# Attention in rounds of two key tiles and units of one query block, with maxima per unit, sums split by engine and four banks of logits

## The chip, the cores and the metric

The kernel runs on one core of a Trainium2 chip. The metric is the device time of one launch in microseconds. TensorE is PE, VectorE DVE, ScalarE ACT, GpSimd POOL and SyncE SP, as in the profile; DMAs are issued by SP, ACT or POOL.

## The reference

The whole is a two-layer decoder: a gated-DeltaNet layer, a shared projection of K, V and forget gates, and a forgetting-attention layer (batch 1, 2048 tokens, width 1024). The change lies in the attention of the second layer, 16 heads of 64:

```python
for blk in range(seq // B_BLOCK):
    s0 = blk * B_BLOCK
    s1 = s0 + B_BLOCK
    logits = (jnp.einsum('bhqd,bhkd->bhqk', q[:, :, s0:s1], k[:, :, :s1]).astype(jnp.float32)
              + log_f_cum[:, :, s0:s1, None] - log_f_cum[:, :, None, :s1])
    causal = jnp.arange(s0, s1)[:, None] >= jnp.arange(s1)[None, :]
    p = jax.nn.softmax(jnp.where(causal, logits, -jnp.inf), axis=-1)
    outs.append(jnp.einsum('bhqk,bhkd->bhqd', p.astype(v.dtype), v[:, :, :s1]))
o = jnp.concatenate(outs, axis=2).transpose(0, 2, 1, 3).reshape(bsz, seq, B_W)
return (o * jax.nn.silu(z)) @ w_out
```

## The kernel before

The program is a row of stages, each ending in a barrier of all engines: DeltaNet projection (pa), delta rule (dr), output projection (oa), the K/V projection (pk), the query projection (pb), the attention (at) and the last output projection (ob). The function `attention` is the attention stage. It works on 8 pairs of heads. For a pair, logits are computed transposed, 128 keys on the partitions by up to 512 queries: a tile is one key tile (kb) against one query block (qb of 4). A pair has 40 tiles (16 + 12 + 8 + 4), and each is done for both heads: 640 exact logits in all.

An exact logit (`exact_logits`, lines 1977 to 1986) is two float32r matmuls (L1983 with the high parts, the gates and minus the maximum as extra rows; L1986 with the low parts) and, on the diagonal, a bf16 mask matmul (L1985). ACT takes the exponential (L2123) into `probs`. One step later PE multiplies the probabilities with V (`sum_values`, L1997): float32 matmuls that fill 64 columns each, one head on each half; the trace shows four records per tile. The denominators are sums over key tiles, added up on DVE (even tiles and all of block 0: L2059, L2062) and POOL (odd tiles: L1870, L1873), joined on DVE (L2069), and then summed over the partitions by PE with a matrix of ones (`sum_tiles`, L2010). ACT inverts them by logarithm and exponential (L2128, L2130). DVE multiplies the output with the gate Z (L2076) and with the inverse (L2081).

The maximum that is subtracted is a rough one. `rough_logits` (L1948, mask L1951) computes queries by keys from the high parts only, 80 of them per pair, each up to 128 x 512, and DVE reduces each to a column of `partial` (L1960). When all 80 are there, DVE reduces them to `top` (L1965), PE turns it (L1971), ACT negates it (L1975) and POOL places it as a row of Q1 by two DMAs (L1855).

The order of the work is written out by hand. In every step j (one tile) each engine does its part of tile j or a few before. `max_steps` spreads the 80 rough logits of the next pair over steps 6 to 33 of the present one: one after each head's exact logits, the rest after the values. For the first pair all 80 run before the main loop (`alone`), and they may use the banks of `logits` as well. The banks of PSUM are: logits 2, rough 2, o 2, total 1, top_turned 1. `probs` holds three tiles. Blocks go from the last (qb = 3) to the first. SP loads a pair's K, Q, V and Z in four blocks of 512 tokens, each block in a group of loads for the rough logits (`load_one`, `load_gates`, L1889 and L1893) and one for the rest (`load_two`, L1904); pair p + 2 takes over the buffers of pair p block by block once that block is gated.

Of the kernel before, what the change touches and what calls it, by code (L numbers as in the profile page):

```python
# [12 lines left out]

# [14 lines left out]
P = 128  # L28
# [3 lines left out]
BLK = 512  # L32
# [1728 lines left out]
def attention(nc, s_K, s_Fp, s_V, s_Q, s_ZT, s_u2T):  # L1761

# [10 lines left out]
    MAIN = [(qb, kb) for qb in reversed(range(NB)) for kb in range(NQ * (qb + 1))]  # L1773
    MAXI = [(qb, h, sub, grp) for qb in range(NB) for h in range(2) for sub in range(NQ) for grp in range(qb + 1)]
    STEPS, MAXS = len(MAIN), len(MAXI)
    ENDS = [j for j in range(STEPS) if j == STEPS - 1 or MAIN[j][0] != MAIN[j + 1][0]]

    ON_POOL = [(j, h) for j in range(STEPS) for h in range(2) if MAIN[j][0] and MAIN[j][1] % 2]
    ON_DVE = [(j, h) for j in range(STEPS) for h in range(2) if (j, h) not in ON_POOL]
    MAX_START, MAX_END = 6, STEPS - 6  # L1780
    with Stage(nc, "at") as st:
# [5 lines left out]
        probs = st.sb("probs", [P, 3, 2, BLK])  # L1787
        sum_v, sum_g = st.sb("sum_v", [P, 2, 2, BLK]), st.sb("sum_g", [P, 2, BLK])
        partial = st.sb("partial", [P, 2, NT, NB])
        top = st.sb("top", [P, 2 * NT])  # L1790
        minus_top = st.sb("minus_top", [2 * NT, P], F32R)
        inv, u = st.sb("inv", [P, BLK]), st.sb("u", [P, 2, BLK])
# [5 lines left out]
        top_in = st.pool_sem("top_in")  # L1798
        consts = st.sem("consts")
        rows_set = [st.sem(f"rows_set{s}") for s in range(2)]  # L1800
        ev = lambda n, per, credit=0: Event(st, n, per, credit)
        logits_ok, probs_ok, pv_ok = ev("logits_ok", 2 * STEPS), ev("probs_ok", 2 * STEPS, 2), ev("pv_ok", STEPS, 3)
        v_summed, g_summed = ev("v_summed", len(ON_DVE), 6), ev("g_summed", len(ON_POOL))
        joined, total_ok = ev("joined", 2 * (NB - 1), 2), ev("total_ok", NB, 2)
# [7 lines left out]
        def over_pairs(body):  # L1812

            for p in range(PAIRS):
                body(p, p // 2, p % 2, p < PAIRS - 1)
# [11 lines left out]
        def _(pool):  # L1827
# [20 lines left out]
            for s in range(2):  # L1848
                pool.sem_inc(u_stored[s], 16)
# [351 lines left out]
```

## Time and profile before

| what | value |
|---|---|
| median of 3 runs | 3534.41 us (3532.44 to 3536.05) |
| the profiled execution's own time | 3540.65 us |
| its span in the trace | 3539.0 us |
| attention stage in it, about | 2417 to 3322 us |
| main loop of the attention, first exact logits to last sum over partitions | 2482 to 3315 us |
| granted clock of TensorE over the span | 0.949 of full speed |

The profile is one execution of the program. Times in its timeline are microseconds from the span's start. "Busy" of PE counts from a matmul's start to its modelled end, and matmuls overlap, so the distance from one start to the next tells more than the length. An engine's idle time stands before the instruction that ended it, with what released it.

### The profile page before, as it was taken

Reading aid. Unit: us, or ns where it says so; the run is one execution under the profiler, and the core shown is the slowest. Engines: PE = TensorE matmul, PEld = TensorE weight load, DVE = VectorE, ACT = ScalarE, POOL = GpSimd, SP = SyncE. Lnnn points to the kernel's source line nnn. Section 1 sums busy time; section 2 is a strip of 40 time slices with the busy share of each in tenths; the row PEclk is TensorE's granted clock in tenths of the full one; section 3 lists DMA queues with packets and bytes.
Section 4 is the critical chain, followed back from the end, with each engine's and each line's share of the span. In section 5 each row is a group of like instructions: output and inputs, shape, how many; then the busy total and the mean of one; then the engine's idle time right before and its main releaser. Section 6 shows DMA issues by size and latency. Waiting matters only on the chain. (4 is left out here: it accounts for less than half of the span.)

```text
span 3539.0 us, 41132 instructions
## 1 busy us (share of the span) xinstructions
PE 3193.6 (90%) x15158; PEld 2315.6 (65%) x15158; DVE 1756.8 (50%) x2771; ACT 1218.3 (34%) x2078; POOL 940.8 (27%) x739
## 2 busy tenths in 40 slices
PE   5889899999978997978999699996999999999798
PEld 4666566888867886866888578884444444444476
DVE  4454444566645665544211142115676777675433
ACT  4344445444414453224111131110344444444311
POOL 0578860233235440100000000001333333333210
PEclk8999899999989998988999899996999999999899
DMA  5233422567555654555431244317243433330333
GB/s 204 74 118 101 131 91 61 187 209 223 177 154 192 200 182 147 180 163 158 119 83 48 87 145 116 107 48 173 60 108 81 108 84 79 81 84 10 110 128 119
DMA packets 270102, 436.35 MB, mean 123 GB/s; under 512 B 73214, under 2 KB 170118, under 8 KB 259612
## 3 DMA queue, kind: packets, MB, share of 16 engines
q1 hardware_dynamic: 230812, 332.18, 31.8%
q0 software_dynamic: 23520, 86.21, 7.8%
q10 hardware_dynamic: 15600, 15.73, 1.5%
q8 instruction: 101, 1.65, 0.2%
q14 instruction: 69, 0.57, 0.1%
HBM read 283.10 MB, written 150.82 MB: 123 GB/s over the span
## 5 line engine op out<-in xcount | busy, mean ns | idle before, releaser
L2123 ACT ACTIVATE at_probs<-at_logits 128x512 f32<-128x512 f32 (+3 forms) x640 | 331.2, 532 | 414.0 <-PE at_logits L1986 381.7
L173 PE MATMUL pa_y<-pa_h_high,pa_w_high 128*128 128x512 f32 x1056 | 422.6, 400 | 7.5 <-ACT pa_acc L839 5.5
L1960 DVE TENSOR_REDUCE at_partial<-at_rough 128x1 f32<-128x512 f32 (+1 forms) x600 | 349.8, 605 | 129.1 <-PE at_rough L1948 76.3
L174 PE MATMUL pa_y<-pa_h_low,pa_w_high 128*128 128x512 f32 x1056 | 413.0, 391 | 0.0
L175 PE MATMUL pa_y<-pa_h_high,pa_w_low 128*128 128x512 f32 x1056 | 412.7, 391 | 0.0
L1873 POOL TENSOR_TENSOR at_sum_g<-at_sum_g,at_probs 128x512 f32<-128x512 f32 (+2 forms) x240 | 251.0, 1063 | 381.1 <-ACT at_probs L2123 380.0
L1997 PE MATMUL at_o<-at_probs,at_V 128*64 128x512 f32 (+3 forms) x1280 | 305.2, 555 | 2.9 <-ACT at_probs L2123 2.9
L1948 PE MATMUL at_rough<-at_K,at_Q 66*128 66x512 f32 (+1 forms) x600 | 250.1, 423 | 30.4 <-DMA at_K<-s_Fp 22.4
L1983 PE MATMUL at_logits<-at_Q,at_K 67*128 67x512 f32 (+3 forms) x640 | 260.9, 408 | 13.4 <-DMA at_Q<-at_minus_top 8.4
L1986 PE MATMUL at_logits<-at_Q,at_K 128*128 128x512 f32 (+3 forms) x640 | 254.0, 397 | 0.0
L173 PE MATMUL pk_y<-pk_h_high,pk_w_high 128*128 128x512 f32 x544 | 218.4, 401 | 30.4 <-POOL pk_ident L98 27.9
L173 PEld LDWEIGHTS pa_y<-pa_h_high,pa_w_high 128*128 128x128 f32 x1056 | 199.5, 189 | 59.8 <-issue 12.3
L173 PE MATMUL pb_y<-pb_h_high,pb_w_high 128*128 128x512 f32 x512 | 204.8, 400 | 35.9 <-POOL pb_ident L98 31.6
L1948 PEld LDWEIGHTS at_rough<-at_K,at_Q 66*128 66x128 f32 x600 | 117.6, 197 | 181.2 <-DVE at_partial L1960 142.2
L174 PEld LDWEIGHTS pa_y<-pa_h_low,pa_w_high 128*128 128x128 f32 x1056 | 199.5, 189 | 43.9 <-issue 3.8
L175 PEld LDWEIGHTS pa_y<-pa_h_high,pa_w_low 128*128 128x128 f32 x1056 | 199.3, 189 | 42.1
L175 PE MATMUL pk_y<-pk_h_high,pk_w_low 128*128 128x512 f32 x544 | 217.3, 399 | 0.0
L174 PE MATMUL pk_y<-pk_h_low,pk_w_high 128*128 128x512 f32 x544 | 217.3, 399 | 0.0
L1983 PEld LDWEIGHTS at_logits<-at_Q,at_K 67*128 67x128 f32 x640 | 123.2, 192 | 135.5 <-ACT at_probs L2123 89.2
L2062 DVE TENSOR_TENSOR at_sum_v<-at_sum_v,at_probs 128x512 f32<-128x512 f32 (+3 forms) x288 | 164.5, 611 | 92.9 <-ACT at_probs L2123 92.9
L174 PE MATMUL pb_y<-pb_h_low,pb_w_high 128*128 128x512 f32 x512 | 204.3, 399 | 0.0
L175 PE MATMUL pb_y<-pb_h_high,pb_w_low 128*128 128x512 f32 x512 | 204.2, 399 | 0.0
(348 smaller groups left out, 5685.8 us busy)
## 6 DMA issues: line engine op xcount, KB each, us to landing
at_Q<-s_Q SPq DMA_DIRECT2D x96, 256.0 KB, 6.8
s_qkv<-pa_sil POOLq DMA_DIRECT2D x16, 1024.0 KB, 6.6
pa_sil<-s_qkv SPq DMA_DIRECT2D x16, 1024.0 KB, 6.3
dr_kv<-s_qkv SPq DMA_DIRECT2D x16, 1024.0 KB
s_K<-pk_parts SPq DMA_DIRECT2D x32, 512.0 KB, 8.0
s_Q<-pb_parts SPq DMA_DIRECT2D x32, 512.0 KB, 8.0
at_K<-s_K SPq DMA_DIRECT2D x32, 512.0 KB, 5.7
pa_wraw<-in_a_w_in_dram ACTq DMA_DIRECT2D x15, 1024.0 KB
```

What stands on the lines that cost most here:

```text
L173: nc.tensor.matmul(out, w_high[:, k], h_high[:, k], start=k == 0, stop=False)
L174: nc.tensor.matmul(out, w_high[:, k], h_low[:, k], start=False, stop=False)
L175: ins = nc.tensor.matmul(out, w_low[:, k], h_high[:, k], start=False, stop=k == KC - 1)
L1873: ins = g.tensor_tensor(sum_g[:, h, off:BLK], sum_g[:, h, off:BLK], x, ALU.add)
L1948: ins = nc.tensor.matmul(bank[:, 0:width], Q1[s][0:DH + 2, h, q_at], K1[s][0:DH + 2, h, grp * BLK:grp * BLK + width], start=True, stop=grp ...
L1960: reduced.done(nc.vector.tensor_reduce(partial[:, h, qb * NQ + sub, grp:grp + 1], rough_bank(j, alone)[:, 0:width], AX.X, ALU.max))
L1983: nc.tensor.matmul(out, K1[s][0:DH + 3, h, k_at], Q1[s][0:DH + 3, h, q_at], start=True, stop=False)
L1986: logits_ok.done(nc.tensor.matmul(out, K2[s][:, h, k_at], Q2[s][:, h, q_at], start=False, stop=True))
L1997: ins = nc.tensor.matmul(o[at, m % 2, off:BLK], V[s][:, kb, at], probs[:, j % 3, h, off:BLK], start=kb == 0, stop=kb == NQ * (qb + 1) - 1)
L2062: ins = v.tensor_tensor(to, to, x, ALU.add)
L2123: probs_ok.done(nc.scalar.activation(probs[:, j % 3, h, off:BLK], logits[:, h, off:BLK], ACT.Exp))
```

## The change

`attention` is rewritten. The unit of work is one query block of one pair (32 units, `UNITS`): the pair 0 goes from block 0 to block 3, the others from 3 to 0. A unit is made of rounds of two key tiles (160 rounds). In a round PE computes the four exact logits (two tiles by two heads), each in a bank of its own, and then the values of the round before, eight records without anything between. The maxima are those of a unit, not of a pair: after a unit's last rough logit they are reduced to `top`, turned into the bank of `total` (there is none for `top_turned` any more), negated, and placed by ACT with two DMAs. Only the eight rough logits of unit 0 run ahead. A planner's loop (`ROUGHS`) spreads the others over the rounds so that a unit's are done four rounds before it starts, as evenly as their due times allow; they stand behind the exact logits in up to four groups. Head 0 is summed on DVE, head 1 on POOL, both tiles of a round; a unit's first two tiles are added directly. The partition sum takes head 0 from `sum_v` and head 1 from `sum_g`, so nothing is joined. `o` has one bank instead of two and `inv` two buffers instead of one. The last product (`normalize`) moves from DVE to POOL. In the stage's start, the rows of ones are filled in parts, and SP issues the first blocks' loads in the order of their use.

```diff
-    MAIN = [(qb, kb) for qb in reversed(range(NB)) for kb in range(NQ * (qb + 1))]
-    MAXI = [(qb, h, sub, grp) for qb in range(NB) for h in range(2) for sub in range(NQ) for grp in range(qb + 1)]
...
-    MAX_START, MAX_END = 6, STEPS - 6
+    UNITS = [(p, qb) for p in range(PAIRS) for qb in (range(NB) if p == 0 else reversed(range(NB)))]
+    START = [0]
+    for _, qb in UNITS:
+        START.append(START[-1] + 2 * (qb + 1))
...
+    ITEMS = [(u, h, sub, grp) for u, (_, qb) in enumerate(UNITS) for h in range(2) for sub in range(NQ) for grp in range(qb + 1)]
+    FIRST = 2 * NQ
+    ITEM_END = [2 * NQ * sum(qb + 1 for _, qb in UNITS[:u + 1]) for u in range(len(UNITS))]
+
+    ROUGHS, DONE = [], FIRST
+    for R in range(ROUNDS):
+        due = [(ITEM_END[u] - DONE, max(START[u] - 4, 0)) for u in range(1, len(UNITS)) if ITEM_END[u] > DONE]
+        take = max([-(-n // (d - R + 1)) for n, d in due if d >= R], default=0)
+        ROUGHS.append(range(DONE, DONE + take))
+        DONE += take
+    TURN = {u: 1 + next(R for R in range(ROUNDS) if ITEM_END[u] - 1 in ROUGHS[R]) for u in range(1, len(UNITS))}
...
-        logits, rough = st.ps("logits", [P, 2, BLK]), st.ps("rough", [P, 2, BLK])
-        o = st.ps("o", [P, 2, BLK])
-        total, top_turned = st.ps("total", [P, BLK]), st.ps("top_turned", [P, BLK])
+        logits, rough = st.ps("logits", [P, 4, BLK]), st.ps("rough", [P, 2, BLK])
+        o, total = st.ps("o", [P, BLK]), st.ps("total", [P, BLK])
...
+            for R in range(ROUNDS + 3):
+                for u in ended(R, 2):
+                    normalize(u)
+                if R < ROUNDS:
+                    add_up(R)
...
+            for n in range(NB):
+                load_one(sp, 0, n)
+                if n < 2:
+                    sp.wait_ge(rows_k, n + 1)
+                load_gates(sp, 0, n)
+                if n:
+                    load_two(sp, 0, n - 1)
...
+                fetch = [] if p + 2 >= PAIRS else [qb] if p else reversed(range(NB)) if qb == NB - 1 else []
...
+            def sum_values(R):
+                u = UNIT_OF[R]
+                p, qb = UNITS[u]
+                if R == START[u]:
+                    gated.wait(pe, u - 1)
+                probs_ok.wait(pe, 4 * R + 3)
+                for t, kb, off in tiles(R):
                     for h in range(2):
...
+            for R in range(ROUNDS + 2):
+                if R < ROUNDS:
...
+                    if R == START[u]:
+                        for n in range(qb + 1):
+                            pe.wait_ge(two_in[p % 2][n], (p // 2 + 1) * TWO)
+                        pe.wait_ge(top_in, 32 * (u + 1))
+                    part = -(-len(items) // 4)
+                    for t, kb, off in tiles(R):
+                        for h in range(2):
+                            exact_logits(R, t, kb, off, h)
+                            for j in items[(2 * t + h) * part:(2 * t + h + 1) * part]:
...
+                                rough_logits(j)
+                for summed in ended(R, 1):
+                    sum_tiles(summed, turned)
+                if 1 <= R <= ROUNDS:
+                    sum_values(R - 1)
+                for turned in turned_in(R):
+                    turn_top(turned, summed)
...
+            for R in range(ROUNDS + 2):
+                for u in ended(R, 1):
+                    gate(u)
+                if R < ROUNDS:
+                    items, first = ROUGHS[R], R == START[UNIT_OF[R]]
+                    half = 2 * -(-len(items) // 4)
+                    for j in items[:half]:
+                        reduce(j)
+                    if not first:
+                        add_up(R, 0)
+                    for j in items[half:]:
+                        reduce(j)
+                    if first:
+                        first_two(R)
+                    else:
+                        add_up(R, 1)
...
+                for h in range(2):
+                    act.dma_start(Q1[p % 2][DH + 2:DH + 3, h, columns(qb)].bitcast(F32), minus_top[h * NQ:(h + 1) * NQ].bitcast(F32))\
+                       .then_inc(top_in, 16)
...
+                    if R >= 2:
+                        pv_ok.wait(act, R - 2)
+                        v_summed.wait(act, ADDED[R - 2] - 1)
+                        g_summed.wait(act, ADDED[R - 2] - 1)
```

PE's order before, two steps with rough logits in the middle of a pair (at_logits exact, at_rough rough, at_o values):

```order
L1997 MATMUL at_o<-at_probs,at_V 64x512 x2
L1948 MATMUL at_rough<-at_K,at_Q 128x512
L1983 MATMUL at_logits<-at_Q,at_K 128x512
L1986 MATMUL at_logits<-at_Q,at_K 128x512
L1948 MATMUL at_rough<-at_K,at_Q 128x256
L1951 MATMUL at_rough<-at_mask_q,at_ident_b 128x128
L1983 MATMUL at_logits<-at_Q,at_K 128x512
L1986 MATMUL at_logits<-at_Q,at_K 128x512
L1948 MATMUL at_rough<-at_K,at_Q 128x512
L1997 MATMUL at_o<-at_probs,at_V 64x512 x2
```

PE's order in the change, from the last exact logit of a unit's second round on:

```order
L1960 MATMUL at_logits<-at_Q,at_K 128x512
L1963 MATMUL at_logits<-at_Q,at_K 128x512
L1948 MATMUL at_rough<-at_K,at_Q 128x128
L1951 MATMUL at_rough<-at_mask_q,at_ident_b 128x128
L1988 MATMUL at_total<-at_sum_v,at_ones 64x512
L1988 MATMUL at_total<-at_sum_g,at_ones 64x512
L1974 MATMUL at_o<-at_probs,at_V 64x512 x4
L1994 MATMUL at_total<-at_ident,at_top 8x128
L1960 MATMUL at_logits<-at_Q,at_K 128x512
```

The values of one tile stood between the exact logits of two steps; now those of two tiles stand together, with the partition sums ahead of them and the turned maxima behind.

DVE's order before, in steps with rough logits (at_partial reductions, at_sum_v adds of both heads of every other tile):

```order
L1960 TENSOR_REDUCE at_partial<-at_rough 128x1 x2
L2062 TENSOR_TENSOR at_sum_v<-at_sum_v,at_probs 128x512 x2
L1960 TENSOR_REDUCE at_partial<-at_rough 128x1 x5
L2062 TENSOR_TENSOR at_sum_v<-at_sum_v,at_probs 128x512 x2
L1960 TENSOR_REDUCE at_partial<-at_rough 128x1 x6
```

DVE's order in the change, the rounds at the start of a unit:

```order
L2039 TENSOR_REDUCE at_partial<-at_rough 128x1 x4
L2054 TENSOR_TENSOR at_sum_v<-at_probs 128x512
L2070 TENSOR_TENSOR at_u<-at_o,at_Z 128x512
L2039 TENSOR_REDUCE at_partial<-at_rough 128x1 x2
L2062 TENSOR_TENSOR at_sum_v<-at_sum_v,at_probs 128x512
L2039 TENSOR_REDUCE at_partial<-at_rough 128x1 x2
L2062 TENSOR_TENSOR at_sum_v<-at_sum_v,at_probs 128x512
```

An add of one head stands between the second and the third reduction of every round, and another behind the fourth.

## Rows read from the trace of the kernel before

**Rows 1.** The page, busy time, share of the span and instructions of each engine.

```profile
PE 3193.6 (90%) x15158; PEld 2315.6 (65%) x15158; DVE 1756.8 (50%) x2771; ACT 1218.3 (34%) x2078; POOL 940.8 (27%) x739
```

**Rows 2.** Three stretches: length, busy time of each engine, granted clock, DMA share, GB/s.

```profile
2440.00:2450.00 10.00, 10.00 (x28) 5.86 (x26) 10.00 (x20) 0.00 (x0) 0.00 (x0) 0.50 1.09 273
2482.00:2500.00 18.00, 17.79 (x57) 7.82 (x57) 5.06 (x10) 8.04 (x14) 6.25 (x6) 0.78 0.42 100
2605.00:3220.00 615.00, 602.75 (x2770) 298.13 (x2769) 450.93 (x811) 264.62 (x505) 213.02 (x219) 1.00 0.32 80
```

**Rows 3.** Timeline of PE, one step: start, length, line, tiles, count.

```profile
2602.02 0.50 PE L1983 MATMUL at_logits<-at_Q,at_K 67*128 67x512 f32 x1
2602.36 0.40 PE L1986 MATMUL at_logits<-at_Q,at_K 128*128 128x512 f32 x1
2602.60 0.40 PE L1983 MATMUL at_logits<-at_Q,at_K 67*128 67x512 f32 x1
2602.83 0.40 PE L1986 MATMUL at_logits<-at_Q,at_K 128*128 128x512 f32 x1
2603.17 1.08 PE L1997 MATMUL at_o<-at_probs,at_V 128*64 128x512 f32 x4
2604.18 0.50 PE L1983 MATMUL at_logits<-at_Q,at_K 67*128 67x512 f32 x1
```

**Rows 4.** Timeline of PE, values followed by the sum over partitions.

```profile
3270.07 1.08 PE L1997 MATMUL at_o<-at_probs,at_V 128*64 128x512 f32 x4
3270.97 1.03 PE L2010 MATMUL at_total<-at_sum_v,at_ones 128*64 128x512 f32 x4
```

**Rows 5.** Timeline of PE, one rough logit between two exact ones.

```profile
3213.27 0.40 PE L1948 MATMUL at_rough<-at_K,at_Q 66*128 66x512 f32 x1
3213.51 0.40 PE L1983 MATMUL at_logits<-at_Q,at_K 67*128 67x512 f32 x1
```

**Rows 6.** Timeline of PE, the turned maxima of the last two pairs that have them.

```profile
3115.70 0.28 PE L1971 MATMUL at_top_turned<-at_ident,at_top 128*32 128x128 f32 x1
...
3222.47 0.28 PE L1971 MATMUL at_top_turned<-at_ident,at_top 128*32 128x128 f32 x1
```

**Rows 7.** Timeline of PE, the wait in the third step of a block.

```profile
3234.03 0.50 PE L1983 MATMUL at_logits<-at_Q,at_K 67*128 67x512 f32 x1 [0.72 <-ACT at_probs L2123]
```

**Rows 8.** Groups of the stage by shape: count, busy us, mean ns, idle before.

```profile
L1960 DVE TENSOR_REDUCE at_partial<-at_rough 128x1 f32<-128x512 f32 x420 | 280.5, 685 | 86.0 <-PE at_rough L1948 76.3 <-PE at_rough L1951 7.7
...
L2123 ACT ACTIVATE at_probs<-at_logits 128x512 f32<-128x512 f32 x448 | 258.9, 596 | 284.1 <-PE at_logits L1986 272.8 <-DVE at_sum_v L2059 0.5
...
L1873 POOL TENSOR_TENSOR at_sum_g<-at_sum_g,at_probs 128x512 f32<-128x512 f32 x144 | 182.6, 1288 | 239.3 <-ACT at_probs L2123 239.3
...
L2062 DVE TENSOR_TENSOR at_sum_v<-at_sum_v,at_probs 128x512 f32<-128x512 f32 x192 | 128.3, 708 | 68.4 <-ACT at_probs L2123 68.4
```

**Rows 9.** Timeline, POOL adds and the VectorE product beside them.

```profile
2643.26 2.52 POOL L1873 TENSOR_TENSOR at_sum_g<-at_sum_g,at_probs 128x512 f32<-128x512 f32 x2 [5.93 <-ACT at_probs L2123]
...
2644.97 1.36 DVE L2081 TENSOR_TENSOR at_u<-at_u,at_inv 128x512 f32<-128x512 f32 x1
```

**Rows 10.** Timeline, the stage's start until the first exact logits.

```profile
2425.80 1.16 SPq L1893 DMA_DIRECT2D at_K<-s_Fp  x4
...
2429.80 0.45 PE L1948 MATMUL at_rough<-at_K,at_Q 66*128 66x128 f32 x1 [22.45 <-DMA at_K<-s_Fp]
...
2473.43 0.40 PE L1971 MATMUL at_top_turned<-at_ident,at_top 128*32 128x128 f32 x1 [1.79 <-DVE at_top L1965]
...
2482.21 0.76 PE L1983 MATMUL at_logits<-at_Q,at_K 67*128 67x512 f32 x1 [8.39 <-DMA at_Q<-at_minus_top]
```

**Rows 11.** Timeline of PE, the last sum over partitions.

```profile
3315.28 1.08 PE L2010 MATMUL at_total<-at_sum_v,at_ones 128*64 128x512 f32 x4
```

**Rows 12.** Timeline of VectorE, the first of its two fills with ones.

```profile
2418.02 3.47 DVE L2047 MEMSET at_K<- 3x4096 f32 x1 [53.67 <-PEq L56]
```

**Rows 13.** DMAs of the maxima (line 1855), from issue to landing.

```profile
DMA to landing us min/median/max: 1.7/1.8/7.0
```

More of the change, by code:

```diff
@@ L14 @@
+import itertools
 import math
@@ L1826, in _, with tiles, columns @@
+        def tiles(R):
+            r = R - START[UNIT_OF[R]]
+            qb = UNITS[UNIT_OF[R]][1]
+            return [(t, 2 * r + t, max(0, 2 * r + t - qb * NQ) * P) for t in range(2)]
+        def columns(n):
+            return slice(n * BLK, (n + 1) * BLK)
         @block.gpsimd
@@ new lines, in _ @@
+            load_two(sp, 0, NB - 1)
+            for n in range(NB):
+                load_one(sp, 1, n)
+            sp.wait_ge(rows_next, 2)
+            for n in range(NB):
+                load_gates(sp, 1, n)
+            for n in range(NB):
+                load_two(sp, 1, n)
+            for u, (p, qb) in enumerate(UNITS):
+                fetch = [] if p + 2 >= PAIRS else [qb] if p else reversed(range(NB)) if qb == NB - 1 else []
+                for n in fetch:
+                    gated.wait(sp, u)
+                    for part in (load_one, load_gates, load_two):
+                        part(sp, p + 2, n)
+                u_ok.wait(sp, u)
+                sp.dma_start(s_u2T[p * P:(p + 1) * P, columns(qb)], u_buf[:, u % 2]).then_inc(u_stored[u % 2], 16)
@@ new lines, in free_total, with sum_tiles @@
+            def free_total(u, turned):
+                logged.wait(pe, u)
+                minus_ok.wait(pe, turned)
+            def sum_tiles(u, turned):
+                v_summed.wait(pe, ADDED[START[u + 1] - 1] - 1)
+                g_summed.wait(pe, ADDED[START[u + 1] - 1] - 1)
+                free_total(u - 1, turned)
+                for h, x in enumerate((sum_v, sum_g)):
+                    ins = nc.tensor.matmul(total[h * DH:(h + 1) * DH], ones[:, :], x[:, u % 2], start=True, stop=True)
+                total_ok.done(ins)
@@ new lines, in add_up, with gate @@
+            def add_up(R, t):
+                u, n = UNIT_OF[R], ADDED[R] - ADDS[R]
+                off = tiles(R)[t][2]
+                probs_ok.wait(dve, 4 * R + 2 * t)
+                v_summed.wait(dve, n + t - 1)
+                to = sum_v[:, u % 2, off:BLK]
+                v_summed.done(v.tensor_tensor(to, to, probs[:, R % 2, t, 0, off:BLK], ALU.add))
+            def gate(u):
+                p, qb = UNITS[u]
+                pv_ok.wait(dve, START[u + 1] - 1)
+                dve.wait_ge(two_in[p % 2][qb], (p // 2 + 1) * TWO)
+                if u >= 2:
+                    dve.wait_ge(u_stored[u % 2], 16 * (u // 2))
+                gated.done(v.tensor_tensor(u_buf[:, u % 2], o[:, :], Z[p % 2][:, columns(qb)], ALU.mult))
@@ L2103, in _ @@
         @block.scalar
         def _(act):
+            a = nc.scalar
             act.preload_act_table_set("natural_log_exp_and_others")
[L2106 to L2133 removed]
```

431 lines of the change are left out of this document (162 added, 269 removed).

## The prediction

> **What bounds the kernel now.** The page comes first: PE is busy for 90% of the span, no other engine for more than half [rows 1]. The change touches the attention stage alone, so the stretches come next. In steady state the granted clock is 1.00 (2.4 GHz) and PE is busy 602.75 of 615 us, idle 2%, while DVE is busy 73%, ACT 43% and POOL 35% [rows 2]. That PE is busy need not mean that it does useful work, so the third view is the timeline of PE: what is the distance from start to start? The first float32r logit after the values takes 0.34 us to the next start, the second and third 0.24 and 0.23, the last one before the values 0.34, the four value matmuls 1.01 [rows 3]. Values that are followed by more float32 work on half the columns take 0.90 [rows 4]. So each passage into the values and back costs (0.34 - 0.24) + (0.34 - 0.24) + (1.01 - 0.90) = 0.31 us that no wait explains; I take 0.30, since the distances are read to 0.01. A pair with rough logits takes 3222.47 - 3115.70 = 106.77 us [rows 6]. The stage's main loop is bound by PE's order of work, not by a wait. Its prologue isn't: for 80 rough logits PE runs at a clock of 0.50 (1.2 GHz) and DVE is busy without a gap, 20 reductions in 10 us [rows 2].
>
> **Part 1, rounds of two tiles.** There are 40 tiles per pair and 8 pairs, so 320 passages now, and 160 with two tiles' values standing together (the order shows x4 where x2 stood). 160 x 0.30 = **-48 us**, all of it on PE. Sums over partitions that now stand behind a rough logit have edges of their own; always standing ahead of the values they have none. I estimate half of the 32, 16 x 0.30 = **-5 us**. The matmuls themselves are as many as before.
>
> **Part 2, four banks for logits.** PE waits 0.72 us for ACT in the third step of a block [rows 7], once per pair by the repeating pattern. With four banks a logit waits for the exponential four back, which in a round of about 5 us is long done: ACT needs 4 x 0.60 = 2.4 us [rows 8]. 8 x 0.7 = **-6 us**. The 12 us of idle PE in 615 [rows 2] bound what all waits together give: 17 us over the loop's 833 us [rows 10, 11].
>
> **Part 3, the start.** Now the first rough logit starts at 2429.80, some 4 us after the gates' transfers are issued at 2425.80; these stood behind two fills of 3.47 us on DVE [rows 10, 12]. A fill of a quarter of that row takes 0.9 us, and the loads of block 0 need about 6 us from 2417: first rough logit at about 2425. Eight of them with their reductions take 5 us at this clock (0.50 us each [rows 2], plus the start). Turning, negating and placing the maxima takes 8.8 us, 2473.43 to 2482.21, with the queues full [rows 10], and they will be full again. So the first exact logits start at about 2439, not 2482.2: **-43 us**. The 72 rough logits that are no longer in front are now PE's work inside: 0.24 us each [rows 5], about 0.25 with those that need a mask: **+18 us**. The planner's loop, worked through, puts 16, 12, 12, 6, 6, 5, 5, 5, 5 of them into the first nine rounds and then 4 per round up to round 137. Rounds 0 to 2 are therefore bound by DVE: 40 reductions and 6 adds, near 27 us, and round 2 waits for the maxima of unit 1, turned only at the end of round 1, another 8.8 us. Round 3 runs at the low clock still: the clock came back about 8 us after dense work began ((1 - 0.78) x 18 / 0.5 = 8 us at the lower level [rows 2]). That is 46 us for four rounds whose content on PE at the full clock is 27 us (6.4 for the two rounds of unit 0, 8.0 for two full ones, 46 x 0.25 for the rough logits, 0.9 for a sum over partitions); the present start loses 4 us in that way. **+15 us**. Rounds with 5 or 6 rough logits put two behind one logit and so wait about 1 us for a bank: **+6 us**. The start as a whole gives -4 us only.
>
> **Part 4, one bank for o and smaller units.** The maxima are turned 32 times, not 8: 24 x 0.1 us (from the 0.04 to the next start and the 0.28 of length [rows 6] as bounds): **+2 us**. The single bank of o makes the first values of a unit wait for the gate of the last. The gate's turn on DVE comes right after the previous values end, and PE has a whole round of logits ahead of these values, 3 us or more against a product of 0.7: nothing on the path; uncovered it would cost 32 x 0.7 = 22 us. ACT now issues the transfers of the maxima and waits for the turn at a round's end; that delays its next exponential by about 1.5 us and is covered by the 2.6 us that ACT has free per round (uncovered: 31 x 1.5 = 46 us). Between DMAs of 1.8 us median [rows 13] and the maxima's three rounds of lead nothing waits after round 6. SP fetches pair 2 once unit 3 is gated, 8 MB in about 35 us, for rough logits 8 rounds (40 us) later: just in time. The tail gets **+1 us**: POOL's product takes 1.29 us [rows 8] for DVE's 0.7.
>
> **Part 5, sums by engine.** DVE gets head 0 and POOL head 1 of every tile. By count DVE gains: no joins, no final product. But timing changes. In the trace a DVE product with two SBUF inputs that starts at 2644.97, while POOL's adds run until 2645.78, ends at 2646.33: it takes 1.36 us instead of 0.68, and ends 0.55 after POOL [rows 9]. All 28 rows of such DVE operations with more than 0.72 us per instruction lie beside a POOL add. The Trainium skill, "SBUF — State Buffer", section "SBUF: two separate sides", says that the pair of ports which VectorE and GpSimd share is an exclusive lock, held for the whole instruction, and that a VectorE operation with two SBUF inputs takes it. By that rule, the trace agrees, each add that meets one of POOL's would wait out its rest. In a full round with 4 rough logits PE needs 8 x 0.24 + 4 x 0.25 + 4 x 0.45 + 0.30 = 5.0 us; DVE needs 4 reductions at 0.50 [rows 2] to 0.55 and 2 adds at 0.7 [rows 8], 3.5 us. Followed step by step, the first add starts while POOL sums the first tile of head 1 and waits about 1 us, the second finds POOL idle: 4.5 us, under 5.0. The unknown is bounded by 0 and by two full waits of 1.27 per round, which would make DVE's round 6.0 us. I take a small toll, **+6 us**.
>
> Sum: -48 - 5 - 6 - 43 + 18 + 15 + 6 + 2 + 1 + 6 = **-54 us**, against the profiled execution's 3540.65 us (3539.0 in its span). The median of the runs is 6 us lower, 3534.4, so the prediction is 3534.4 - 54 = **3480 us**. A measurement of this kernel can tell about 0.2%, 7 us, from no change.
>
> **The rivals.**
> - *The clock stays low in the start.* While DVE sets the pace in the first rounds PE may not count as dense, as it didn't for 50 us in the prologue [rows 2]. If it stays at 0.50 to round 10, some 45 us of content take about 25 us more, since part of it waits anyway: 3505 us. For: rounds of 5 and 6. Against: these rounds are bound by PE at the low clock. 0.14.
> - *The passage isn't what the distances say.* If only entering and leaving are saved and the two tiles' values cost 1.01 each (rows 4 have other weights behind the values, not another tile's), each round saves 0.20: 32 us less 48 is 16 us lost: 3496 us. 0.10.
> - *Better than the sum.* The rounds of the start overlap more, the waits of PE vanish altogether (17 us instead of 6) and the toll of part 5 is zero: 3463 us. 0.15.
> - *The shared port makes DVE the bound: slower.* It decides from a mean wait of (5.0 - 3.5) / 2 = 0.75 us per add; 54 us are eaten up over 130 rounds at 0.4 more per round, so at 0.95. With 1.15 per add the round is 5.8 us, 130 x 0.8 = 104 us: 3584 us. PE would then wait for rough banks. For: POOL now works in every round, with two adds of 1.27 [rows 8]. Against: a wait of DVE gives POOL time to finish, so two full waits in each round don't hold together. 0.06.
> - *No change*, by the start turning out 40 us worse: 0.03.
>
> **The numbers.** The forecast, 3470 to 3495 us, has 0.52. Faster by over 0.2%: 0.52 + 0.14 + 0.10 + 0.15 = 0.91, same 0.03, slower 0.06. The range for 8 in 10 reaches from the better case to beyond the first rival: 3459 to 3515 us.
>
> **What the profile will show.** The four value matmuls as one group of eight per round, 1.9 us from start to next start, and 160 of them; pairs that take 98 to 99 us between their qb = 3 units instead of 106.77; first exact logits near 2439; the clock at 0.50 until about 2482; DVE adds of two lengths, near 0.65 and up to 1.9; PE's idle under 2% after round 9. The forecast is wrong if pairs take more than 102 us: then either the passages kept their price, or PE waits for reductions behind adds that POOL holds. It is also wrong if the clock is low beyond 2500.

## The result and the profile after

The changed kernel takes 3478.27 us (median of 4 runs, 3476.47 to 3482.47) against 3535.23 us of the kernel before on the same chip (4 runs, 3532.44 to 3538.62): ratio 0.984, 95% interval 0.9823 to 0.9857. That is 57 us less; 54 us less and 3480 us were forecast.

The page's busy line stands to [rows 1] so: PE's busy time falls by 60 us and the span by 58, so its share stays at 90%; POOL has 99 us more to do.

```profile
PE 3133.1 (90%) x15182; PEld 2334.9 (67%) x15182; DVE 1769.4 (51%) x2659; ACT 1226.4 (35%) x2102; POOL 1039.4 (30%) x764
```

Stretches of the kernel after, with the columns of [rows 2] (length, busy us of PE, PEld, DVE, ACT, POOL with counts, granted clock, DMA share, GB/s): rounds 0 and 1, the wait for the maxima of unit 1, rounds 2 and 3, then the clock's rise, then the steady part.

```profile
2434.24:2448.51 14.27, 12.52 (x36) 7.76 (x37) 7.74 (x15) 2.17 (x4) 1.28 (x2) 0.50 1.09 249
2448.51:2462.54 14.03, 12.39 (x38) 6.67 (x37) 9.30 (x19) 1.32 (x4) 1.18 (x2) 0.51 1.08 213
2462.54:2470.53 7.99, 0.28 (x3) 0.11 (x2) 0.00 (x0) 0.27 (x1) 0.00 (x0) 0.69 1.09 249
2470.53:2483.92 13.39, 11.96 (x32) 6.89 (x32) 7.76 (x14) 2.39 (x4) 1.26 (x1) 0.50 1.10 255
2483.92:2494.28 10.36, 10.36 (x31) 5.35 (x29) 5.96 (x10) 3.61 (x6) 3.26 (x3) 0.57 0.17 39
...
2480.00:2490.00 10.00, 9.64 (x28) 5.86 (x27) 7.42 (x14) 2.39 (x4) 2.53 (x2) 0.50 0.61 136
2490.00:2500.00 10.00, 9.90 (x40) 4.11 (x41) 5.52 (x9) 4.16 (x8) 4.16 (x4) 0.86 0.07 27
2600.00:3150.00 550.00, 542.49 (x2705) 303.35 (x2703) 434.49 (x698) 264.79 (x515) 274.19 (x229) 0.99 0.39 97
```

The stage's start in the timeline, against [rows 10] and [rows 12]: the first fill, the first rough logit, the maxima of unit 0 turned and landed, a rough logit that waits for a reduction, the maxima of unit 1 turned and landed.

```profile
2413.73 0.91 DVE L2029 MEMSET at_Q<- 3x1024 f32 x1 [53.04 <-PEq L57]
...
2418.53 0.45 PE L1948 MATMUL at_rough<-at_K,at_Q 66*128 66x128 f32 x1 [14.85 <-DMA at_K<-s_Fp]
...
2425.02 0.37 PE L1994 MATMUL at_total<-at_ident,at_top 128*8 128x128 f32 x1 [1.08 <-DVE at_top L2043]
...
2434.24 0.77 PE L1960 MATMUL at_logits<-at_Q,at_K 67*128 67x512 f32 x1 [8.85 <-DMA at_Q<-at_minus_top]
2436.88 1.01 PE L1948 MATMUL at_rough<-at_K,at_Q 66*128 66x512 f32 x2 [0.55 <-DVE at_partial L2039]
...
2462.54 0.27 PE L1994 MATMUL at_total<-at_ident,at_top 128*8 128x128 f32 x1
...
2470.53 0.76 PE L1960 MATMUL at_logits<-at_Q,at_K 67*128 67x512 f32 x1 [7.72 <-DMA at_Q<-at_minus_top]
```

The steady part in the timeline of PE, against [rows 3] and [rows 6]: values of two tiles as one group, 1.86 us from start to next start where two groups took 2 x 1.01; the turned maxima of the same unit of two pairs and, between them, a wait of 0.76 us for a reduction; the last sum over partitions.

```profile
2605.53 1.94 PE L1974 MATMUL at_o<-at_probs,at_V 128*64 128x512 f32 x8
2607.39 0.50 PE L1960 MATMUL at_logits<-at_Q,at_K 67*128 67x512 f32 x1
...
2664.99 0.27 PE L1994 MATMUL at_total<-at_ident,at_top 128*8 128x128 f32 x1
...
2671.63 0.50 PE L1948 MATMUL at_rough<-at_K,at_Q 66*128 66x512 f32 x1 [0.76 <-DVE at_partial L2039]
...
2763.00 0.27 PE L1994 MATMUL at_total<-at_ident,at_top 128*8 128x128 f32 x1
...
3253.70 0.59 PE L1988 MATMUL at_total<-at_sum_v,at_ones 128*64 128x512 f32 x1
```

The groups by shape, against [rows 8]: VectorE's and GpSimd's adds have become longer, 1112 and 1394 ns where they took 708 and 1288.

```profile
L2062 DVE TENSOR_TENSOR at_sum_v<-at_sum_v,at_probs 128x512 f32<-128x512 f32 x168 | 186.7, 1112 | 9.2 <-ACT at_probs L2127 8.8
...
L1873 POOL TENSOR_TENSOR at_sum_g<-at_sum_g,at_probs 128x512 f32<-128x512 f32 x168 | 234.1, 1394 | 167.6 <-ACT at_probs L2127 160.0
```

**Where the time went.** The stages ahead vary by some us between executions, so I count from the last matmul of the projection ahead of the stage (2406.9 before, 2403.3 after). The first exact logits come 31.0 us behind it instead of 75.3: -44.3. From them to the last sum over partitions, "the loop" below, it is 3253.70 - 2434.24 = 819.5 us instead of 3315.28 - 2482.21 = 833.1: -13.6. Together -57.9. In the loop a pair, measured at its turned maxima, takes 97.4, 98.0, 98.0, 99.7, 98.0, 99.2 us, mean 98.4, instead of 106.8.

The fourth and the sixth of these pairs are longer because the granted clock falls in them. In the fourth PE waits 0.77 us for a reduction, and from about 2868.3 to 2871.8 the clock is 0.50; the sixth has the same from about 3066.3 to 3069.7. The other pairs have waits of the same length and the clock stays at 1.00. In slices of 5 us the loop loses 3.4 us behind the rise at 2493 by this (time in a slice times 1 minus its clock), 1.7 in each of the two pairs; the loop of the kernel before has no such slice.

```profile
2867.62 0.50 PE L1948 MATMUL at_rough<-at_K,at_Q 66*128 66x512 f32 x1 [0.77 <-DVE at_partial L2039]
...
2869.00:2871.00 2.00, 2.00 (x7) 0.77 (x8) 0.99 (x3) 0.00 (x0) 0.21 (x1) 0.50 0.92 231
3067.00:3069.00 2.00, 2.00 (x6) 0.47 (x4) 0.65 (x2) 0.42 (x1) 0.00 (x0) 0.50 0.94 214
```

### The profile page after: what moved, and what is told of

Its sections match the earlier page's. It is cut to its first block and busy times, and to the rows that moved or that the text cites. A ratio compares the mean times of both kernels' runs of the same rounds, so it can differ in the third digit from the quotient of the medians.

```text
span 3480.9 us, 40912 instructions
## 1 busy us (share of the span) xinstructions
PE 3133.1 (90%) x15182; PEld 2334.9 (67%) x15182; DVE 1769.4 (51%) x2659; ACT 1226.4 (35%) x2102; POOL 1039.4 (30%) x764
## 5 line engine op out<-in xcount | busy, mean ns | idle before, releaser
L2039 DVE TENSOR_REDUCE at_partial<-at_rough 128x1 f32<-128x512 f32 (+3 forms) x640 | 372.1, 605 | 186.3 <-PE at_rough L1948 142.0
L1873 POOL TENSOR_TENSOR at_sum_g<-at_sum_g,at_probs 128x512 f32<-128x512 f32 (+3 forms) x256 | 301.2, 1177 | 241.9 <-ACT at_probs L2127 230.1
L1948 PE MATMUL at_rough<-at_K,at_Q 66*128 66x512 f32 (+3 forms) x640 | 248.2, 396 | 29.7 <-DMA at_K<-s_Fp 14.8
L1974 PE MATMUL at_o<-at_probs,at_V 128*64 128x512 f32 (+3 forms) x1280 | 270.7, 544 | 0.0
L2062 DVE TENSOR_TENSOR at_sum_v<-at_sum_v,at_probs 128x512 f32<-128x512 f32 (+3 forms) x256 | 232.7, 909 | 10.7 <-ACT at_probs L2127 10.0
L638 DVE SCALAR_TENSOR_TENSOR pa_acc<-pa_ybuf,pa_taps,pa_acc 128x2048 f32<-128x2048 f32 x72 | 198.3, 2755 | 2.6
L1960 PEld LDWEIGHTS at_logits<-at_Q,at_K 67*128 67x128 f32 x640 | 125.0, 195 | 106.5 <-issue 89.1
```

What stands on the lines that cost most here:

```text
L638: ins = v.scalar_tensor_tensor(acc[:, :], x, w, acc[:, :], ALU.mult, ALU.add)
L1873: g_summed.done(g.tensor_tensor(to[:, off:BLK], to[:, off:BLK], xs[:, t, off:BLK], ALU.add))
L1948: ins = nc.tensor.matmul(bank[:, 0:width], Q1[p % 2][0:DH + 2, h, q_at], K1[p % 2][0:DH + 2, h, grp * BLK:grp * BLK + width], start=True, ...
L1960: nc.tensor.matmul(out, K1[s][0:DH + 3, h, k_at], Q1[s][0:DH + 3, h, q_at], start=True, stop=False)
L1974: ins = nc.tensor.matmul(o[at, off:BLK], V[p % 2][:, kb, at], probs[:, R % 2, t, h, off:BLK], start=kb == 0, stop=kb == NQ * (qb + 1) - 1)
L2039: reduced.done(v.tensor_reduce(partial[:, u % 2, h * NQ + sub, grp:grp + 1], rough[:, j % 2, 0:width], AX.X, ALU.max))
```

## The experiments

Each kernel ran beside the kernel before on the same chip. "Ratio" is against that, with its 95% interval. Each is the changed kernel with the edit shown, unless said otherwise; "..." stands for lines left out. "The window" is 2600 to 3150 us of the profiled execution. The first ones take the change apart.

**e1_split: values apart again.** Each tile's four value matmuls stand alone, the first tile's between the logits of the next round's two tiles.

```diff
-            def sum_values(R):
+            def sum_values(R, part):
...
-                for t, kb, off in tiles(R):
+                for t, kb, off in tiles(R)[part:part + 1]:
...
+                        if t == 0 and R >= 1:
+                            sum_values(R - 1, 0)
...
-                    sum_values(R - 1)
+                    sum_values(R - 1, 1)
```

> The changed kernel, but the values of the two tiles of a round stand apart again: tile 0's behind the first two exact logits of the next round, tile 1's behind the last two. Banks, sums and start as in the change. Theory (the passage into the values and back costs PE 0.30 to 0.34 us each time): 160 more passages, 48 to 54 us more, and up to 15 us for the single bank of o, since the gate of the last unit then has only half a round ahead of it; 3526 to 3548 us, pairs 105 us instead of 98. Rival (the gain comes from four banks and from waits that are gone, the joining itself is free): under 3490 us, pairs below 100 us.

Measured: 3529.74 us (10 runs), ratio 0.9981 (0.9972 to 0.9991). Nearly the whole gain is gone, as the theory had it. The loop is 871.8 us, pairs average 105.0. Part of that is not passages: PE waits for the gating product, as PE's waits in the window show (us in total, times, longest).

```profile
PE at_o L1974 <- DVE at_u L2075: 14.4, 15, 1.3
```

**e2_two_banks: logits in two banks, values joined.**

```diff
-                probs_ok.wait(pe, l - 4)
-                out = logits[:, l % 4, off:BLK]
+                probs_ok.wait(pe, l - 2)
+                out = logits[:, l % 2, off:BLK]
...
```

> The changed kernel with two banks for exact logits instead of four (a logit waits for the exponential two back). Theory (banks were worth a few waits for ACT): with a rough logit behind each exact one the distance of 0.72 us just covers the exponential of 0.60, so 5 to 15 us more, 3483 to 3493 us. Rival (four banks carry the gain, since four logits in a row outrun ACT): each round waits 0.5 us or more, 3540 us or more.

Measured: 3528.91 us (9 runs), ratio 0.998 (0.997 to 0.9991); the loop is 874.4 us. Both expectations miss: beside joined values the banks are worth 50 us, where 6 were forecast for them. PE's waits, same window:

```profile
PE at_logits L1960 <- ACT at_probs L2127: 20.6, 21, 1.1
PE at_rough L1948 <- DVE at_partial L2039: 7.8, 13, 0.9
```

And PE loses time also where no wait is shown. In this piece of its timeline the logit at 2709.86 stands 0.16 behind a mask (it is 0.04 where nothing holds it) and then takes 0.34 to the next start instead of 0.31:

```profile
2709.70 0.23 PE L1951 MATMUL at_rough<-at_mask_q,at_ident_b 128*128 128x128 bf16 x1
2709.86 0.50 PE L1960 MATMUL at_logits<-at_Q,at_K 67*128 67x512 f32 x1
2710.20 0.39 PE L1963 MATMUL at_logits<-at_Q,at_K 128*128 128x512 f32 x1
```

Of 141 full-width first parts of a logit that follow a rough logit directly in this window, 34 take over 0.29 us to the next start here, none of 152 in the changed kernel. The clock takes its part too: it falls behind waits four times and twice stays at 0.50 for about 10 us. By slices of 5 us the loop loses 13.7 us in this way, the changed kernel's 3.4, so some 10 of the 55 us that this loop is longer are the clock.

```profile
2632.00:2640.00 8.00, 8.00 (x23) 4.76 (x23) 5.69 (x8) 2.99 (x6) 3.44 (x3) 0.50 0.56 161
```

**e7_split_two_banks: both undone.** The edits of e1 and e2 together; with the changed kernel this closes the square.

> e1_split and e2_two_banks together: values of the two tiles apart, two banks for exact logits. Each of them alone cost 50 us. Theory (the four banks are what lets values be joined: two logits in a row fit into two banks, four don't): the values between give ACT its time, so no more than e1_split alone, 3524 to 3540 us. Rival (passage and banks are two separate costs that add): 3570 us or more.

Measured: 3537.47 us (10 runs), ratio 1.0009 (0.9998 to 1.002), as the theory had it; loop 882.5 us, pairs average 106.5, as before the change. The earlier start is still in this kernel, and its 44 us go into the loop, with the 72 rough logits that moved there and the long first rounds. So all other parts of the change together (start, maxima per unit, split sums, one bank for o) give nothing that the runs can tell from zero. Against this kernel the joining alone gives 8.6 us (e2), the banks alone 7.7 (e1), both 59; taken by the ratios, since the kernels ran on different chips, it is 10, 10 and 60. Neither part is worth much without the other.

**e3_no_pool_sums: no adds on GpSimd.** Small fills stand in their place (a unit's first add is a fill of the same width), so the denominators of head 1 are left out.

```diff
-                        g_summed.done(g.tensor_tensor(to[:, off:BLK], to[:, off:BLK], xs[:, t, off:BLK], ALU.add))
+                        g_summed.done(g.memset(to[:, BLK - 1:BLK], 1.0))
...
```

> The changed kernel without POOL's adds of head 1: each is a small fill instead, so the sums of head 1 and what is divided by them are not the reference's. Theory (DVE's adds wait for POOL at the shared port, 1.11 us instead of 0.65, but DVE has slack in the round): the adds fall to 0.65 us and the time by 0 to 6 us, 3472 to 3478 us. Rival (DVE is at its limit and PE waits for it in each round): 20 us or more less, 3458 us or below.

Measured: 3471.17 us (4 runs), ratio 0.9805 (0.9784 to 0.9827), loop 807.7. That is 1 us below the theory's range and far above the rival's. The median is 7 us below the changed kernel's and the two intervals overlap; the loops of the two traces are 12 us apart. Pairs take 96.2 us, each alike, PE is busy 549.96 of 550 us, and the clock does not fall (window, and the group of VectorE's adds, now 683 ns):

```profile
2600.00:3150.00 550.00, 549.96 (x2769) 309.90 (x2768) 383.04 (x717) 270.29 (x526) 58.40 (x235) 1.00 0.40 100
...
L2062 DVE TENSOR_TENSOR at_sum_v<-at_sum_v,at_probs 128x512 f32<-128x512 f32 x168 | 114.8, 683 | 9.9 <-ACT at_probs L2127 9.5
```

**e8_split_no_pool: values apart, no adds on GpSimd.** The edits of e1 and e3 together.

> Edit: values of the two key tiles apart again (as in e1_split) and the head sums of GpSimd left out by memsets (as in e3_no_pool_sums; its partition sums are then of ones, so the output is another). What it tells: in the changed kernel leaving out GpSimd's additions gave 7 to 10 us; with values apart TensorE has 40 passages in a pair and pairs of 104.8 us, so VectorE has 7 us more room in each. Theory (passages alone set the pair there, 0.33 us each, and the additions of GpSimd cost only where VectorE is short of room): 3522 to 3530 us, pairs of 103 to 105 us. Rival (the additions cost VectorE, and so TensorE, the same in either form): 7 to 10 us less than e1_split's 3529.7, so 3519 to 3522 us; if the waits for the gating product in e1_split (17.4 us in all) were GpSimd's doing, 3512 us or less.

Measured: 3517.27 us (4 runs), ratio 0.9949 (0.9933 to 0.9966), loop 856.3, pairs 102.4. This lies in none of the expected ranges, 2 us below the rival's and 5 above the 3512 that would have put all the waits down to GpSimd. GpSimd's adds cost e1 12 us by the medians and 15.5 in the loop; the joined form 7 and 12. With them out, the waits for the gating product fall from 14.4 to 1.3 us. What is left tells the price of a passage with little wait mixed in: PE is busy 547.67 of the 550 us of the window, and 549.96 in e3, a difference of 0.4 us per pair. The turned maxima of one unit in two following pairs, here and, below, in e3:

```profile
2677.11 0.27 PE L1995 MATMUL at_total<-at_ident,at_top 128*8 128x128 f32 x1
...
2779.53 0.27 PE L1995 MATMUL at_total<-at_ident,at_top 128*8 128x128 f32 x1
```

```profile
2670.59 0.27 PE L1994 MATMUL at_total<-at_ident,at_top 128*8 128x128 f32 x1
...
2766.82 0.27 PE L1994 MATMUL at_total<-at_ident,at_top 128*8 128x128 f32 x1
```

102.42 - 96.23 = 6.19 us for 20 groups of values fewer: **0.31 us per passage**, 0.29 without that idle time; over the loop (856.3 - 807.7) / 160 = 0.30.

**e9_three_first: VectorE's first add behind three quarters of the reductions.**

```diff
-                    half = 2 * -(-len(items) // 4)
+                    half = 3 * -(-len(items) // 4)
```

> The changed kernel with DVE's first add of a round behind three of the four groups of reductions instead of two (the bound half = 3 * ... for 2 * ...). Theory (the add meets POOL's add of the same tile at the shared port and holds back the third reduction, on whose bank PE waits; without POOL pairs take 96.2 us instead of 98.2): the third reduction no longer stands behind it, pairs fall to 96.3 to 97.3 us and the time by 7 to 14 us, 3465 to 3473 us. Rival (what PE waits for is the fourth reduction, or DVE is short as a whole): no change, 3476 us or more.

Measured: 3480.1 us (4 runs), ratio 0.9845 (0.9829 to 0.9862): nothing, as the rival had it. The two waits of 0.75 us per pair were still there (2672.62, 2682.89). So it was not this add that stood in the reductions' way, which led to the next one.

**e12_gate_later: the gating product behind the first half of the reductions.**

```diff
+                items = ROUGHS[R] if R < ROUNDS else []
+                half = 2 * -(-len(items) // 4)
+                for j in items[:half]:
+                    reduce(j)
                 for u in ended(R, 1):
                     gate(u)
                 if R < ROUNDS:
-                    items, first = ROUGHS[R], R == START[UNIT_OF[R]]
-                    half = 2 * -(-len(items) // 4)
-                    for j in items[:half]:
-                        reduce(j)
+                    first = R == START[UNIT_OF[R]]
```

> Edit: on VectorE the gating product of a unit that has ended is done after the first half of the round's reductions, not ahead of them; nothing else. In the changed kernel TensorE waits twice in each pair of heads for 0.76 us for a reduction (at 2671.63 and 2681.89), behind a copy or addition of 1.0 us, the gating product of 0.68 us and the reductions. Theory (the product stands in the way): both waits vanish, 1.2 to 1.5 us per pair of 98 us, six pairs and the ends: 3467 to 3471 us. Rival (the product was not what the reductions waited for, or the values then wait for it): 3475 to 3482 us, the waits move to the value matmuls of the round.

Measured: 3473.76 us (4 runs, 3469.76 to 3477.18), ratio 0.9826 (0.981 to 0.9843): between the two expectations, and by the intervals not certain against the changed kernel. The trace is clear: of the two waits one of 0.15 to 0.19 us per pair is left, pairs take 96.6 us, PE is busy 548.47 of 550, the loop is 808.5 us. The clock does not fall in it any more, so of its 11 us some 3.4 are the clock and 7.6 the waits themselves. These 11 us between two executions are more than the 4.5 between medians (the profiled one was the fastest of its four here, the slowest in the changed kernel); how much holds is open within that.

```profile
2600.00:3150.00 550.00, 548.47 (x2767) 309.18 (x2764) 434.20 (x712) 268.74 (x523) 280.64 (x235) 1.00 0.38 97
```

GpSimd's adds are all still there. So of the 12 us by which the loop of e3 is shorter, these traces put nearly all to this one place, a round behind a unit's start, where a copy or add that GpSimd holds up, the gating product and the reductions stand in a row on VectorE, and to the fall of the clock behind it.

**e11_hold_loads: nothing but the maxima in flight.** SyncE waits for the maxima of unit 0 behind the first loads, and for those of unit 1 ahead of pair 1's.

```diff
                 if n:
                     load_two(sp, 0, n - 1)
+                if n == 1:
+                    sp.wait_ge(top_in, 32)
             load_two(sp, 0, NB - 1)
+            sp.wait_ge(top_in, 64)
```

> Edit: on SyncE's queue a wait for the maxima of unit 0 behind the first block's loads and block 1's first part, and a wait for the maxima of unit 1 ahead of pair 1's loads; nothing else. In the changed kernel TensorE waits 8.85 us (to 2434.24) and 7.72 us (to 2470.53) for two transfers of 2 KB that carry maxima, while the DMA engines are busy at a share of 1.08 to 1.10 with loads that are needed later. Theory (the small transfers stand behind the loads in the DMA engines): each wait falls to some 2 us, first exact logits 6 us earlier, 11 to 13 us in all: 3464 to 3469 us. Rival (the latency is the transfer's own, or what is held back is missed later): the waits stay at 7 to 9 us or new ones for at_K, at_Q come up, 3476 to 3486 us.

Measured: 3465.95 us (4 runs), ratio 0.9802 (0.9786 to 0.9819), as the theory had it. The two waits fall from 8.85 and 7.72 to 3.39 and 2.90 us; the DMA share beside the second is 0.02 instead of 1.09.

```profile
2425.02 0.77 PE L1963 MATMUL at_logits<-at_Q,at_K 67*128 67x512 f32 x1 [3.39 <-DMA at_Q<-at_minus_top]
...
2456.92 0.76 PE L1963 MATMUL at_logits<-at_Q,at_K 67*128 67x512 f32 x1 [2.90 <-DMA at_Q<-at_minus_top]
...
2450.00:2457.00 7.00, 4.10 (x12) 1.11 (x11) 1.04 (x3) 0.27 (x1) 0.00 (x0) 0.50 0.02 7
```

The Trainium skill, "DMA: Bandwidth & Descriptors", section on queues, rings and completion order, says that each DMA engine takes turns between the queues of SyncE and ScalarE packet by packet, and that a semaphore is raised only once every earlier write of that engine, across its queues, has landed. The rows show that the transfer is late while other loads run, not which of the two held it.

**e4, e6, e5: more units' rough logits ahead of round 0.** The changed kernel has as few rough logits ahead of the first exact ones as maxima per unit allow; is that the best? The edit, with AHEAD = 2, 3 and 4 (24, 48 and 80 rough logits ahead); in e5 the rough logits of pair 2 wait until round 29 besides.

```diff
-    FIRST = 2 * NQ
+    AHEAD = 3
...
+    FIRST = ITEM_END[AHEAD - 1]
...
-            for j in range(FIRST):
-                rough_logits(j)
-            pe.wait_ge(consts, 1)
-            turn_top(0, -1)
+            for u in range(AHEAD):
...
+                for j in range(ITEM_END[u - 1] if u else 0, ITEM_END[u]):
+                    rough_logits(j)
+                pe.wait_ge(consts, 1)
+                turn_top(u, -1)
...
```

> The changed kernel with the 24 rough logits of units 0 and 1 ahead of the loop instead of the 8 of unit 0; the maxima of unit 0 are turned after the first 8, those of unit 1 after all 24. Rounds 0 to 2 then hold 8, 8, 8 rough logits instead of 16, 12, 12. Theory (in the start PE stands twice for 8 to 9 us until the DMA of the maxima lands, and rounds 0 and 1 are drawn out to 14 us by reductions): the 16 fit into the first of these waits and the second goes, 12 to 22 us less, 3456 to 3466 us. Rival (the start is bound by the loads or by the reductions' total, wherever they stand): within 5 us of the changed kernel.

> As e4_ahead2, with the 48 rough logits of units 0 to 2 ahead of the loop; then each round has 4 from round 0 on. Theory (in the first rounds PE at the low clock and DVE's reductions draw each other out, so rough logits there cost more than 0.25 us each, about as much as ahead of the loop): the first exact logits 12 us later than with 24, rounds 0 to 8 shorter by 10 to 16 us together; 3456 to 3464 us. Rival (ahead of the loop they cost their full 0.5 us, inside it 0.25): 8 us or more above e4_ahead2, 3470 us or more.

> All 80 rough logits of pair 0 ahead of the loop, as in the kernel before, each unit's maxima turned behind its own, no rough logit of pair 2 before round 29 (its loads come then). Theory (overlapping them with the main loop brought next to nothing, since rounds 0 to 3 took 60 us instead of 27): first exact logits near 50 us after the stage's start instead of 21, and the changed kernel's time within 8 us, 3470 to 3486 us. Rival (the overlap is worth the 43 us by which the first exact logits came earlier, less 18): 3500 us or more.

| | us (4 runs each) | ratio (95%) | first exact logits | loop |
|---|---|---|---|---|
| changed kernel | 3478.27 | 0.984 (0.9823 to 0.9857) | +31.0 | 819.5 |
| e4, 24 ahead | 3462.01 | 0.9785 (0.9765 to 0.9804) | +35.7 | 796.6 |
| e6, 48 ahead | 3454.08 | 0.9762 (0.9746 to 0.9779) | +55.1 | 776.2 |
| e5, 80 ahead | 3489.71 | 0.9865 (0.9849 to 0.9881) | +81.8 | 771.9 |

With 24 ahead, inside the theory's range, the exact logits come only 5 us later, since the new rough logits fill the 9 us in which the maxima travel; the second wait goes too. With 48 ahead, 2 us below the theory's range and far from the rival's, the loop gives back what the start takes and 1 us more by the trace (last sum at +831.3 against +832.3). With 80 the time misses both of its ranges by 4 and 10 us: the loop gives back only 4 of 27 us (what the held rough logits of pair 2 add to that isn't separated). The best is two or three units; three has the lower median, but the intervals of the two overlap.

**e13_ahead3_gate_later: the best of both.** The edits of e6 and e12 together.

> Edits of e6_ahead3 (the 48 rough logits of three units ahead of round 0) and of e12_gate_later (the gating product behind the first half of the reductions) together. e6_ahead3 gave 3454 us and still waits for a reduction twice in a pair (0.65 and 0.54 us); e12_gate_later gave 3474 us against 3478, pairs of 96.6 us in place of 97.4 to 99.7. Theory (the two gains are of different stretches and add up): both waits vanish, pairs of 96.2 to 96.8 us, 3446 to 3451 us. Rival (what e6_ahead3 took out of the rounds had already given VectorE its room): 3452 to 3457 us. The maxima's transfers are not held apart here, since with three units ahead TensorE has work until they land.

Measured: 3449.51 us (5 runs, 3442.39 to 3454.85), ratio 0.9755 (0.9742 to 0.9769), against 3478 of the changed kernel and 3536 of the one before. The theory's range holds. The trace shows both edits at work: pairs in the middle of the loop take 96.2 us, the loop 764.1 instead of e6's 776.2. Of these 12 us, 6.8 are the clock, which falls four times in e6's loop and not once in this one. It is the fastest version here; its lead over e6 in the medians, 4.6 us, is inside the intervals.

```profile
2735.70 0.27 PE L1995 MATMUL at_total<-at_ident,at_top 128*8 128x128 f32 x1
...
2831.87 0.27 PE L1995 MATMUL at_total<-at_ident,at_top 128*8 128x128 f32 x1
```

## Why the prediction was right

The total and the two blocks it is made of are right: the start to the first exact logits -44.3 (forecast -43), the loop -13.6 (forecast -48 - 5 - 6 + 18 + 15 + 6 + 2 + 1 + 6 = -11). Inside the loop two terms were each off by some 15 us, in opposite directions; that they cancel is luck, and without it the total would have been some 15 us off. The terms -5, +18, +2 and +1 and the 6 us of the rounds with 5 or 6 rough logits were not measured by themselves. Term by term:

- **Joined passages, -48: right, beside four banks.** The full-width value groups take 1.86 us each, and e3 against e8 measures 0.29 to 0.31 us per passage, the sum that was read from [rows 3] and [rows 4]: 48.6 us over the loop. With two banks the joining gives 9 to 10 (e7 against e2). The rival that two tiles' values in a row would still cost 1.01 each is out.
- **Four banks, -6: the number right, its place wrong.** With values apart the banks give 7.7 us, what the wait of [rows 7] said. With values joined they give 50: in e2 nearly the whole gain is lost again. The wait was read in an order in which 1.0 us of values stands between logits; with 1.9 us of values in one piece and four logits in one run, PE comes to a bank whose exponential isn't done. Rows show 20.6 us of such waits and 7.8 us for reductions in 550, and the clock that falls behind them costs some 10 us of the loop; what the holds that show as no wait add is seen in single rows and not summed up.
- **Start, -43: right**, its parts within 3 us. The first rough logit came 15.2 us behind the last matmul of the stage ahead, where 2425 - 2406.9 = 18.1 was forecast (the fill took the forecast 0.9 us); turning and placing the maxima took 9.2 us instead of 8.8, and the eight rough logits 6.5 instead of 5.
- **Rounds 0 to 3, +15: this term failed.** Forecast was 46 us, 27 of it for three rounds bound by VectorE's reductions. They took 2494.28 - 2434.24 = 60 us. In rounds 0 and 1 PE was busy 12.5 and 12.4 us of 14.3 and 14.0 at a granted clock of 0.50, VectorE 7.7 and 9.3: PE at 1.2 GHz was the bound, not VectorE; only the other 1.8 and 1.6 us were waits for reductions. Rounds 0 to 2 took 41.7 us without the wait for the maxima, where 27 were forecast: PE's content of these rounds had been priced at the full clock and only round 3 at the low one. The wait for unit 1's maxima was as forecast, 8.0 us against 8.8. The clock was at 0.50 until about 2493 ((1 - 0.86) x 10 / 0.5 = 2.8 us past 2490), not 2482.
- **Steady rounds: better than the sum.** The sum's terms make a pair 106.8 - 6.4 = 100.4 us; the forecast's own line on the profile said 98 to 99, which didn't follow from them. Measured is 98.4, so 8 x 2.0 = 16 us better, which paid for the 14 of the first rounds, and that with 3.4 us of the loop lost to the clock. Without GpSimd's adds, and with PE never idle, a pair takes 96.2 (e3). Of the 10.5 between 106.8 and 96.2, passages are 6.2 and the idle 2% of [rows 2] 2.1; for the rest, 2.2 us per pair, no experiment isolates it.
- **GpSimd's adds, +6: 12 in the loop.** Their way onto VectorE was right and is shown: its add takes 1112 ns beside them and 683 without (e3), which is what the exclusive lock of the shared ports in "SBUF — State Buffer", section "SBUF: two separate sides", of the Trainium skill would do. But the mean delay, 0.43 us, is far from the 0.95 per add from which it would have made the kernel slower, and in an ordinary round of the window PE waits for nothing. It waits behind a unit's start alone.
- **The gate, 0: failed.** It was costed at nothing because the values that wait for it come a whole round later. True of PE's values, and in the changed kernel PE doesn't wait there. But the work queued behind it on VectorE, the first two reductions, is waited for: two waits of 0.75 us in a pair, and twice in the loop the clock falls behind one of them (e12).
- **Clock stays low, 0.14:** it didn't; 2490 to 2500 has 0.86, and from 2500 it is 1.00 but for the two falls. That it falls behind waits in the steady part was not among the rivals.

## What to carry to other kernels

Two edits that are each worth 8 to 10 us alone can be worth 59 together: when one edit lengthens the piece of work between two uses of a buffer, price the buffers for the new order, not by the waits of the old. On an engine that works in order, ask of each instruction not only who waits for its result but who waits for what stands behind it. Look at the granted clock behind every wait of a busy PE: a wait can cost more than its own length. And price early work at the clock that the rows show there: at the low level an engine that seems to have room is the bound, so work is better placed into its waits for transfers (e4, e6) than into its first rounds.

## What the runs showed of the hardware

- A change of PE between logits (float32r, all 128 columns) and values (64 columns) costs 0.29 to 0.31 us there and back that no wait in the profile explains (e3, e8). The Trainium skill, "TensorEngine Tiling (Array Packing)", section "Key Properties", says that changing the tiling mode drains TensorE; the price is this case's, and the runs don't separate it from the change of number format.
- For the maxima, 2 KB per transfer, PE waited 8.9 and 7.7 us while the DMA engines were busy with other loads, 3.4 and 2.9 with those held back (e11).
- Behind waits of PE of 0.5 to 1.2 us the granted clock fell from 1.00 to 0.50 in some places and not in others: twice in the changed kernel's loop, at 1.7 us each, four times in e6's (6.8 us in all), and 13.7 us in e2's. In the loops of e3, e8, e12 and e13, where PE waits for 0.22 us at most at a time in the window, it did not fall.
- GpSimd's adds slow VectorE's by 63% on average (683 to 1112 ns), and yet moving one product of 0.68 us took away 11 of the 12 us that separate the loops with and without them (e12, e3).
